# Gate rows of four norms: from TensorE and ScalarE to a tensor in DRAM

## The reference, cut to what matters

```python
def adaln(cvec, w, b):
    return jnp.split(jax.nn.silu(cvec) @ w + b, 6, axis=-1)

def sublayer(x, shift, scale, gate, g_pre, g_post, fn):
    h = rmsnorm(x, g_pre) * (1 + scale[:, None]) + shift[:, None]
    out, aux = fn(h)
    return x + gate[:, None] * rmsnorm(out, g_post), aux
```

## Time and profile before

| | |
|---|---|
| Time, median of 3 runs | 1456.68 us (1454.04 to 1459.20) |
| Span of the profiled execution | 1455.5 us (its whole time is not listed) |
| Busy: PE, PE weight loads, DVE, ACT, POOL | 95%, 74%, 60%, 51%, 7% |
| Mean granted PE clock | 0.981 of 2.4 GHz |
| DRAM traffic | 358 MB, 246 GB/s in the mean |

### The profile page before, as it was taken

One profiled execution on the slowest core, in us unless ns is written; L12 is line 12 of the kernel. 1 busy time (PEld: TensorE's weight loads), 2 busy tenths in 40 slices (PEclk: granted clock), 3 DMA queues, 4 the chain that ended last, 5 costly groups with the idle time before them and its releaser, 6 DMA issues.

```text
span 1455.5 us, 18974 instructions
## 1 busy us (share of the span) xinstructions
PE 1375.8 (95%) x7338; PEld 1083.7 (74%) x7338; DVE 873.2 (60%) x1184; ACT 749.4 (51%) x978; POOL 97.8 (7%) x170
## 2 busy tenths in 40 slices
PE   7999899899999998999989899999999998899996
PEld 3997557799998877888667677557877743788884
DVE  2533676623334435779675696555966603979796
ACT  3432476622223335497355485445865403768674
POOL 0402420000000000200000200000000000000002
PEclk9999999999999998999999999999999999999998
DMA  9933997633343323233771698667997799999993
GB/s 355 291 140 123 366 350 270 222 116 116 120 151 135 115 88 116 87 116 116 255 280 47 246 399 303 242 229 268 403 340 276 281 387 409 410 383 407 375 378 131
DMA packets 132238, 358.20 MB, mean 246 GB/s; under 512 B 6237, under 2 KB 30201, under 8 KB 132025
## 3 DMA queue, kind: packets, MB, share of 16 engines
q1 hardware_dynamic: 120440, 321.53, 59.9%
q0 software_dynamic: 9344, 32.25, 6.5%
q10 hardware_dynamic: 2368, 3.23, 0.6%
HBM read 335.34 MB, written 22.55 MB: 246 GB/s over the span
## 4 chain that ended last, share of the span: by engine, by line
PE 78%; DVE 10%; DMA 6%; ACT 4%; issue 2%; SPq 1%; DVEq 0%; ACTq 0%
PE bank L2299 29%; PE bank L1948 12%; PE bank L1703 7%; PE bank L1959 6%; PE bank L2247 6%; PE bank L1753 4%; PE bank L1700 3%; DMA ring<-in_moe_w_dram 2%; DMA ring<-in_mod_w_dram 2%; PE bank L1632 2%; PE bank L1678 1%; DMA arena<-in_moe_w_dram 1%; DVE arena L2746 1%; DVE ring_parts L2443 1%; PE bank L2187 1%
## 5 line engine op out<-in xcount | busy, mean ns | idle before, releaser
L2299 PE MATMUL bank<-arena_parts 128*128 128x512 f32 x1072 | 264.0, 393 | 4.6 <-ACT arena_parts L1446 2.6
L2299 PEld LDWEIGHTS bank<-arena_parts 128*128 128x128 f32 x1072 | 200.0, 188 | 54.6 <-issue 11.6
L2986 DVE TENSOR_TENSOR ring_parts<-ring,arena_parts 128x2048 fp32r<-128x2048 f32 x85 | 192.4, 2286 | 78.9 <-PE bank L2247 43.5
L1446 ACT ACTIVATE arena_parts<-ring 128x2048 fp32r<-128x2048 f32 x85 | 162.0, 1917 | 28.1 <-DMA ring<-in_moe_w_dram 22.7
L2299 PE MATMUL bank<-ring_parts,arena_parts 128*128 128x512 f32 x504 | 136.1, 392 | 2.9 <-DVE ring_parts L2986 2.9
L1948 PE MATMUL bank<-ht_parts,arena_parts 128*128 128x384 f32 x352 | 118.2, 336 | 0.9 <-DVE xn_parts L2454 0.8
L1948 PE MATMUL bank<-ht_parts,ring_parts 128*128 128x384 f32 x352 | 117.7, 334 | 0.0
L1948 PE MATMUL bank<-xn_parts,arena_parts 128*128 128x384 f32 x352 | 117.7, 334 | 0.0
L2299 PEld LDWEIGHTS bank<-ring_parts,arena_parts 128*128 128x128 f32 x504 | 94.9, 189 | 23.8 <-DVE ring_parts L2986 4.1
L2681 DVE TENSOR_TENSOR arena<-arena,bank 128x384 f32<-128x384 f32 x22 | 12.2, 554 | 123.7 <-PE bank L1948 123.7
L1703 PE MATMUL bank<-ht_parts,ring_parts 128*128 128x384 f32 x256 | 86.2, 337 | 0.0
(11 more groups left out here) (501 smaller groups left out, 2698.6 us busy)
## 6 DMA issues: line engine op xcount, KB each, us to landing
ring<-in_moe_w_dram SPq DMA_DIRECT2D x144, 1024.0 KB, 7.2
ring<-in_mod_w_dram SPq DMA_DIRECT2D x24, 2048.0 KB, 11.0
arena<-in_moe_w_dram SPq DMA_DIRECT2D x48, 1024.0 KB, 7.2
ring<-in_ff_w_dram SPq DMA_DIRECT2D x23, 1024.0 KB, 7.8
ring<-in_w_in_odd_dram SPq DMA_DIRECT2D x6, 2048.0 KB, 8.0
ring<-in_w_in_even_dram SPq DMA_DIRECT2D x5, 2048.0 KB, 9.6
ring<-in_ff_w_dram SPq DMA_DIRECT2D x5, 2048.0 KB, 8.0
routed<-cst POOLq DMA_DIRECT2D x1, 7168.0 KB, 22.9
```

Source lines behind the costliest of these rows:

```text
L1446: act.activation(whi_moe[high_at(w, n_)], e_half(j, h), ACT.Copy).then_inc(whi_ready, 1)
L2299: ins = pe.matmul(bank[base + b][:, :], lhs[:, c_, :], rhs[:, k, 512 * b:512 * b + 512], start=(first and h == 0 and k == 0 and n_ == 0), ...
L2986: dve.tensor_tensor(e_half(j, h, low=True), e_half(j, h), whi_moe[high_at(w, 2 * j + h)], ALU.subtract).then_inc(wlo_ready, 1)
```

## The change

The gate columns go to a DRAM tensor `gates`, element by element, by two DMAs of ACT for each norm; one DMA of POOL for each norm then reads the two rows back to all 128 partitions of `gb`. `gate_row`, `keep_gate` and their eight calls are gone. ACT's issues stand in the attention loop (i = 6 and 18), in the mLSTM loop (u = 4) and behind the split of `out_proj(1)`'s weights. DVE waits for the broadcast where it uses tile 0 of a norm.

```diff
+        gates = nc.dram_tensor("gates", [4, CONDS, D], F32, kind="Internal").ap()
...
+        gates_out, BIAS_IN = [sem(f"gates_out{s}") for s in range(2)], 16 * (7 + 4)
...
+            def gates_to_all(s):                                   # POOL
+                pool.wait_ge(gates_out[s % 2], 32 * (s // 2 + 1))
+                row = gates[s:s + 1, :, :].rearrange("o c d -> o (c d)")
+                pool.dma_start(gb[:, :, :].rearrange("p c d -> p (c d)"), row.to_broadcast([P, CONDS * D]))\
+                    .then_inc(bias_gates_in, 16)
+            pool.wait_ge(stored, 16 * 4)
+            gates_to_all(0)            # behind the masks
...
+            pool.wait_ge(x_ready, 3)
+            gates_to_all(1)            # behind the issue of the zero fills
...
+            pool.wait_ge(proj_done, index[("o", 2)] + 1)
+            gates_to_all(2)            # before the experts' scatter
+            pool.wait_ge(x_ready, 9)
+            gates_to_all(3)
...
-            def keep_gate(s, c_):                                  # ACT
-                b = gate_bank(s, c_)
-                act.wait_ge(gb_made, 2 * s + c_ + 1)
-                act.activation(gb[:, c_, 0:512], bank[b][:, :], ACT.Copy)
-                act.activation(gb[:, c_, 512:1024], bank[b + 1][:, :], ACT.Copy).then_inc(gb_kept, 1)
+            def gates_to_rows(s):
+                act.wait_ge(gains_ready, s + 1)
                 for c_ in range(CONDS):
+                    act.dma_start(gates[s, c_].rearrange("(k p) -> p k", p=P), gcol[:, s, :, c_],
+                                  allow_slow_non_contiguous=True).then_inc(gates_out[s % 2], 16)
...
-            for c_ in range(CONDS):                                # PE, norm 2
-                pe.wait_ge(ot_dve, HEADS[1] + 2 + c_)
-                gate_row(2, c_)
+            pe.wait_ge(ot_dve, HEADS[1] + 3)
...
+                else:                                              # DVE, add_product, t = 0
+                    dve.wait_ge(bias_gates_in, BIAS_IN + 16 * (s + 1))
```

More of the change, by code:

```diff
@@ L430, in trunk_step @@
         x_in, cst_in, rows_in = sem("x_in"), sem("cst_in"), sem("rows_in")
-        small_in, even_in, bias_in = sem("small_in"), sem("even_in"), sem("bias_in")
+        small_in, even_in, bias_gates_in = sem("small_in"), sem("even_in"), sem("bias_gates_in")
         odd_in, wrg_in, router_in = sem("odd_in"), sem("wrg_in"), sem("router_in")
@@ L804, in _ @@
                               bass.AP(tensor=I["b_rpb"].tensor, offset=(k_ + 4) * 31 + 15,
-                                      ap=[[465, B_HEADS], [-1, GRID_W], [1, GRID_W]])).then_inc(bias_in, 16)
-            pool.wait_ge(bias_in, 16 * 7)
+                                      ap=[[465, B_HEADS], [-1, GRID_W], [1, GRID_W]])).then_inc(bias_gates_in, 16)
+            pool.wait_ge(bias_gates_in, 16 * 7)
             pool.dma_start(wg[:, :, :], cut(I["w_in_odd"][0], 2048, 16)).then_inc(odd_in, 16)
@@ L836, in _ @@
                         bias[64 * half:64 * half + 64, q, :, 0:256].rearrange("p h (r c) -> p h r c", r=4),
-                        shear[:, :, k_:k_ + 4, :].rearrange("h c r k -> c h r k")).then_inc(bias_in, 16)
-            pool.wait_ge(bias_in, 16 * (7 + 4))
+                        shear[:, :, k_:k_ + 4, :].rearrange("h c r k -> c h r k")).then_inc(bias_gates_in, 16)
+            pool.wait_ge(bias_gates_in, BIAS_IN)
             for half in range(2):
@@ L1214, in _ @@
                         ins.then_inc(hsq_ready, 1)
+                if i in (6, 18):
+                    gates_to_rows(i // 12)
                 if i == 20:
@@ L1409, in _ @@
                     mlstm_exp(u + 1)
+                if u == 4:
+                    gates_to_rows(2)
                 if u == 6:
@@ L1432, in _ @@
             head_roots(3, 4)
-            keep_gates(2)
             high_out(1, 1)
@@ L1449, in _ @@
                 high_out(1, n_)
+            gates_to_rows(3)
             for h in range(2):
@@ L1458, in _ @@
             norm_tiles(2)
-            keep_gate(3, 0)
             act.wait_ge(shifts_ready, 5)
@@ L1468, in _ @@
                 ins.then_inc(ht_act, 1)
-            keep_gate(3, 1)
             def xg_hi(w, b):
@@ L1667, in turn_in @@
                 ins.then_inc(xn_turned, 1)
[L1669 to L1680, removed]
             def project(o, p, what, beside=()):
@@ L1738, in out_proj @@
                 for j in range(2):
-                    if m == 0 and t == 0 and j:
-                        gate_row(0, 0)
                     for n in range(4):
@@ L2117, in _ @@
             pe.wait_ge(fin_kept, 1)
-            for c_ in range(CONDS):
-                gate_row(3, c_)
             for k in range(KD):
@@ L2133, in _ @@
             pe.wait_ge(router_in, 32)
-            pe.wait_ge(gb_kept, 7)
+            pe.wait_ge(x_ready, 9)
             for k in range(KD):
@@ L2348, in _ @@
             pe.wait_ge(htok_ready, 6)
-            pe.wait_ge(gb_kept, 8)
             pe.wait_ge(route_ready, PICKED)
@@ L3230, in store_row @@
                                          op0=ALU.mult, op1=ALU.add).then_inc(x_ready, 1)
-            dve.wait_ge(gb_kept, 8)
+            dve.wait_ge(bias_gates_in, BIAS_IN + 16 * 4)
             last = rounds + LOOPED
```

16 lines of the change are left out of this document (removed).

## The result

The change makes the kernel slower: 1483.69 us median of 6 runs (1473.71 to 1485.07) against 1457.94 us for the kernel before beside it (1454.04 to 1460.69). The ratio is 1.0159, 95% interval [1.0142, 1.0177]. The forecast was 1448.2 us, with 1443 to 1455 as its range; rival 3, the 4 B stores that hold the DMA engines, given 0.08 and sized at 1476, is in outline what happened. The profiled execution has a span of 1482.8 us, 27.3 more than before.

What follows compares the result with a forecast made beforehand. The prediction took TensorE (PE), busy 95% of the span, as the bound. It summed -4.2 (A) + 0 (B) - 1.8 (C) - 3.7 + 1.2 (D) + 0 (E) = -8.5 us, giving 1448.2 us, range 1443.0 to 1455.0.

Steps and rivals of the forecast that it cites:

- rival 3: Attention and mLSTM loops: 4 B stores hold the DMA engines, 15 us for a norm, +19, 1476 us; chance 0.08.
- the price of the column stores: Time the gate-column stores to DRAM hold the DMA engines: 1.0 us for a norm, between 0 and 5.8.
- the wait for a panel in the attention loop: Sign that the forecast is wrong: PE waits for a weight panel in the attention loop; no size given.
- 4 B packets of more than 60 ns each: Sign that the forecast is wrong: the column stores' packets each take more than 60 ns.
- the floor that the page's section Bandwidth gives: Column stores: about 0.67 us for 64 pieces on an engine, 1.3 for a norm, 0.1 more in the sum.
- Place A: Out projection of layer 0, 235 to 245 us: two gate calls and a PE wait go, 4.2 us gained.
- Place B: Gate call near 267 us, within PE's wait for a norm: nothing gained, cost 0 to 1.5, taken as 0.
- Place C: Gate call at 296.4 us within the up projection's matmuls: 1.8 us gained, nothing to take its place.
- Place D: Norm 2, 751.8 to 772 us: two calls and a wait go, 3.7 gained; 1.2 lost to a late panel.
- The panel of row 23: Modulation weights before norm 2, no slack: lands 3.7 us later behind the broadcast and stores; 1.2 lost, between 0 and 5.
- Place E: Norm 3, 798.4 to 806 us: a gate call goes but the normed tile is late; -1.0 to +1.0, taken as 0.
- The four broadcasts: POOL's loads of gate rows to SBUF, 2.7 us of all engines each: hidden at norms 0, 1, 3; norm 2 hurts.

Runs made afterwards that it cites:

- repaired version: Against the changed kernel: DVE turns gate columns in 32 x 32 blocks, POOL stores 64 pieces of 128 B for a norm, ACT issues none; 1452.30 us, ratio 0.9957.

## Why the prediction was wrong

The step that failed is the price of the column stores, one term: "Between nothing and 2.9 for each DMA, 0 to 5.8 for a norm, I take 1.0." It measured 15.1 for norm 0 in the changed kernel and 8.9 for norm 2. The price came from `wg`, 1024 pieces of 64 B that landed in 2.9, which is like in number and unlike in three things: it is a load, its pieces are 16 times as large, and it was issued at 63.9, where the DMA share is 0.43 (63.8 to 67.0) and not 1.05. The runs show two things that decide: with number and size held, the loss comes and goes with the spacing, and without saturated reads around them packed stores cost no time that can be seen. Whether small loads would behave so is untested. The upper bound fell with it: 5.8 was an end only for pieces like `wg`'s.

Rival 3 had the mechanism in outline (the streams of two loops are held), its 15 us for a norm, and nearly its total (1476 against 1483.7). The total is in part luck: from the table the attention loop lost 15.5 where it said 14, the mLSTM loop (row 16 to row 23) 11.2 where it said 15, and 5.7 more went between the first output projection and norm 1's transposes, which it didn't have. It had the price at each piece; by the runs it is at pieces that stand closely packed. I gave it 0.08 on the strength of `wg`, and that is the second fault: the row that carried the sum was also the only evidence against the rival, so a wrong choice of row did both. Rival 3 itself says that the sign turns at 5.4 us for a norm, within the bounds of 0 to 5.8 that I had set, and yet slower had a chance of 0.09. Of the signs that I had named, the wait for a panel in the attention loop was the right one; "4 B packets of more than 60 ns each" would have missed it, since their records show 9 ns.

The Trainium skill, DMA: Bandwidth & Descriptors, section Specifications, has pieces under 512 B read, modified and written back. The prediction, by the floor that the page's section Bandwidth gives, let this change the sum by 0.1 us. If the size of a piece set the price, spread and packed ones would cost alike, and they don't: 4 B pieces 16 B or more apart cost less than 1 us of the stream for a norm, and packed ones 13. That read, modify and write is also why neighbours hinder one another is my guess; no run shows it.

The other steps, with the stores out of the way (repaired version against before, from the table):
- Start to row 15, nothing forecast: -0.9, not looked into.
- *Place A*, -4.2 forecast: row 15 to the last matmul of the projection goes from 50.6 to 46.0, -4.6. Right. In the changed kernel ACT waited there for `w_out` panels, landed in 22.3 us and not 9.2.
- *Place B*, 0: from there to the transposes 6.4 and 6.4; from them to the up projection 4.2 and 4.8. Cost 0.6 of the 1.5 allowed.
- *Place C*, -1.8: up projection to row 16, 426.2 and 423.4: -2.8. Right in sign, 1.0 too small; I can't say where the rest is from.
- *Place D*, -3.7 and +1.2: row 23 to the last matmul of the projection goes from 49.4 to 45.1, -4.3. The panel of row 23 costs +2.5 (row 16 to row 23, 41.3 and 43.8), with PE's wait for it 2.5 where it was 0.47. Net -1.8 against -2.5.
- *Place E*, 0: last matmul to router 11.8 and 12.0. Right, +0.2.
- The four broadcasts, hidden but for norm 2: right, by the run without stores.
- Left out: the end. Of the 9.2 us of lead at the router 1.5 go within the experts' stage and 2.9 behind its last matmul: 1.5 because the gathers of the answers don't land earlier by as much as PE is done (the last is issued 7.7 earlier, and what waits for it starts 6.2 earlier), 1.4 because PE starts its product at the lower clock, behind a longer idle stretch.

In sum the forecast of -8.5 was -9.2 at the router, and 6.5 in the time. The mechanism of the gain was right; the cost of the way there was not.

## What to carry to other kernels

Before small pieces are stored to DRAM beside a saturated stream, ask how closely they stand (4 B apart cost 13 us of the stream for a norm here, 16 B apart 0.9): turn the data first (here one 32 x 32 block turn on DVE), store rows of 64 B or more, or issue the store where the streams rest. A DMA's own packets and queue share don't show such a price; look at the GB/s of short windows behind its issue, beside the share. And where no row of a trace shows an operation, the nearest row may set a value, but neither the end of the range nor the chance of the rival that lives on it.

## What the runs showed of the hardware that I had not expected

- 2048 stores of 4 B, packed, among reads at 387 GB/s: the rate falls to 97 to 118 GB/s at an engine share of 0.8 to 1.0, and 13 to 15 us of the stream are lost for norm 0, 8.9 for norm 2; 8, 16, 32 and 512 B apart 2.1, 0.9, 0.3 and 0.2 us. In a quiet stretch the packed ones' packets take 1.5 us, they land in 10.8, and the engines are idle meanwhile.
- A third DMA on ACT's queue, right behind two of 1024 pieces, holds ACT itself for 3.7 to 6.5 us in the attention loop and the mLSTM loop, in all four such runs, and for 0.6 to 1.3 at norm 3; the first two mostly take 0.4 and 0.6.
- DVE reads a tile with a stride of 64 B at 1031 ns for 512 columns, and densely at 688.
